# The triangular inverse of a 128-token chunk, made from its two 64x64 diagonal blocks on opposite quarters of TensorE

## The chip, the cores and the metric

The kernel runs on one core of one Trainium2 chip. The metric is the device time of one execution in microseconds, the median of several runs. The engines of a core are TensorE (PE in the profile; its weight loads are PEld), VectorE (DVE), ScalarE (ACT), GpSimd (POOL) and SyncE (SP), which issues DMAs. Each works through its own list of instructions in order and waits for others by semaphores.

## The reference

One layer of a streaming encoder over 2048 tokens of width 1024: an RMS norm, one wide projection, a gated delta rule (8 heads of width 128, with a short causal convolution and a decay), a sliding-window attention with sinks, their gated merge, an output projection and a last norm. The part that the change touches is the triangular inverse inside the delta rule, per head and per chunk of 64 tokens:

```
n_mat = where(strict_lower, -(kb @ k.T) * decay, 0)
t_mat = eye + n_mat
p_mat = n_mat
for _ in range(log2(CHUNK) - 1):        # CHUNK = 64
    p_mat = p_mat @ p_mat
    t_mat = t_mat + t_mat @ p_mat       # ends as inverse(I - n_mat)
u = t_mat @ vb
w = t_mat @ (kb * exp(gc))
```

A state of 128x128 per head is then carried from chunk to chunk.

## The kernel before

The 2048 tokens are worked on in 4 blocks of 512 (`NB`), a block in 8 heads, a head in 4 chunks of 128 tokens (`NT`, twice the reference's chunk, which gives the same outputs). All weights come as tiles of 128x1024. In block 0 a tile arrives in float32 and is split into a high part (ScalarE, L436) and a low part (POOL, L363); both are saved, and later blocks load them back. A weight product is three passes (L1074 to L1076: high by high, high by low, low by high) for each of eight slices of the contraction.

TensorE's list is written out by hand. While it works on the delta rule and the attention of one head, it also projects the next head's inputs: six weight tiles (q, k and v of the delta rule, the attention's query, two gates) of eight steps each, 48 steps of three matmuls. `fill(n)` in the head's code runs the next n of these steps, and `fill(99)` all that are left. The last head of a block fills with six gate tiles instead. Two PSUM banks (0 and 1) take the projected tiles in turn, so that a tile's first step waits (`z_read`) until the tile two before has been read out of its bank. ScalarE and VectorE have fill steps of their own in their lists, which read these banks: ScalarE copies the projections (L518, L542, L543) and takes the tanh of the gates (L551), VectorE does the convolution (L840, L844) and the SiLU (L826).

A head begins with the sums of decays (L1161), transposes of k, q and v (L1157), and the products k by k and q by k (L1168). VectorE makes the negated strict triangle from k by k, transposed, in `pt_sb[0]` (L886), for four chunks side by side in a 128x512 tile, and adds the identity (L890). After nine fill steps TensorE transposes this (L1225), and ScalarE copies it to `p_sb[0]` (L589). Then come six levels (`LEVELS`). `square(l)` makes the next power of the triangle (L1179) and its transpose (L1183), four 128x128 float32 products each; ScalarE copies both (L589, L595). `accumulate(l)` multiplies the running inverse by that power (L1193), and VectorE adds the result (L905). The attention's logits (L1203), the transposes of its probabilities (L1210) and its values (L1218) stand between the levels, and one or two fill steps between any two of them.

Then the four chunks of 128 tokens are run through the state in order (L1256 to L1272), with fill steps between, and `fill(99)`. In that time VectorE normalizes the head's output (L988) by a power that POOL computes (L376). The head ends when TensorE transposes this output (L1282); `head_dve_done` says that VectorE has gated it. `square_o` (L650) sums the squares of the outputs on ScalarE; for the last chunk it stands ahead of ScalarE's remaining fill steps.

Of the kernel before, what the change touches and what calls it, by code (L numbers as in the profile page):

```python
# [6 lines left out]
P = 128  # L7
# [3 lines left out]
TB = 512  # L11
# [10 lines left out]
LEVELS = 6  # L22
# [77 lines left out]
def build_program(nc, x, w_tiles, norm_w, gdn_norm_w, decay_bias, step_const, bias, final_w, masks, saved, out):  # L100
    with ExitStack() as ctx:
# [79 lines left out]
        p_sb = [chunks(scratch(4)), chunks(scratch(5))]  # L181
        pt_sb = [chunks(scratch(6)), chunks(scratch(7))]
        tt_sb = [chunks(scratch(8)), chunks(scratch(9))]
# [83 lines left out]
        attn_ready = sem("attn_ready")  # L267
        p_done = sem("p_done")
        pt_done = sem("pt_done")
        tt_done = sem("tt_done")  # L270
        p_ready = sem("p_ready")
        pt_ready = sem("pt_ready")
        tt_ready = sem("tt_ready")
        s0_ready = sem("s0_ready")
# [143 lines left out]
        def _(act):  # L418
# [151 lines left out]
            def head(par, n1, fill):  # L570
                n4, n5, n7 = ((n1 - 1) * i for i in (NT, LEVELS - 1, LEVELS + 1))
# [26 lines left out]
                squares(ssq[:, 1, :], bch(3), ssq_ready[1], 1, tt_sb[1])  # L598
                act.wait_ge(dec_done, n1)
                act.activation(dec, bch(5), ACT.Exp).then_inc(dec_ready, 1)  # L600
                squares(ssq[:, 0, :], bch(2), ssq_ready[0], 0, p_sb[1])
                act.wait_ge(ssq_ready[1], n1)
                fill(1)
                p_copy(0)
# [5 lines left out]
                pt_copy(1)  # L610
# [4 lines left out]
                pt_copy(2)  # L615
# [14 lines left out]
                pt_copy(3)  # L630
                softmax_exp(0)
                p_copy(4)
                pt_copy(4)
                p_copy(5)
                pt_copy(5)
                probs_copy(0)
                fill(1)
                p_copy(6)
# [9 lines left out]
                def square_o(t):  # L648
                    act.wait_ge(o_ready, n4 + (t + 1))
                    ins = act.activation(tt_sb[1][:, t, :], o_sb[:, t, :], ACT.Square, accum_out=sso[:, t:t + 1])  # L650
                    if t == NT - 1:
                        ins.then_inc(sso_ready, 1)
# [86 lines left out]
        def _(dve):  # L739
# [122 lines left out]
            def head(b, hh, fill):  # L862
                par, n1 = hh % 2, b * H + hh + 1
                n4, n6, n7 = ((n1 - 1) * i for i in (NT, LEVELS, LEVELS + 1))
# [20 lines left out]
                for t in range(NT):  # L885
                    ins = dve.scalar_tensor_tensor(pt_sb[0][:, t, :], bch(6)[:, t, :], bj[:, t:t + 1], dec_n[:, t, :],  # L886
                                                   ALU.mult, ALU.mult)
                ins.then_inc(pt_ready, 1)
                dve.wait_ge(pt_ready, n6 + 1)
                dve.tensor_tensor(tt_sb[0], pt_sb[0], mk[:, IDENT:IDENT + 1, :].to_broadcast([P, NT, P]), ALU.add  # L890
                                  ).then_inc(tt_ready, 1)
# [56 lines left out]
                add_tt(6)  # L948
# [122 lines left out]
        def _(pe):  # L1071
# [78 lines left out]
            def head(b, par, n1, fill):  # L1150
                n4, n6, n7 = ((n1 - 1) * i for i in (NT, LEVELS, LEVELS + 1))
# [20 lines left out]
                fill(9)  # L1172
# [13 lines left out]
                def accumulate(l):  # L1186
# [3 lines left out]
                    if l == 1:  # L1190
                        pe.wait_ge(attn_ready, n1)
# [258 lines left out]
```

## Time and profile before

| | |
|---|---|
| Median of 3 runs | 3073.92 us (3073.32 to 3075.18) |
| Profiled execution | 3076.6 us |
| Its span, first to last instruction | 3074.8 us |
| TensorE matmul busy | 2972.8 us, 97% |
| TensorE weight load busy | 2541.9 us, 83% |
| VectorE busy | 1401.3 us, 46% |
| ScalarE busy | 1052.9 us, 34% |
| POOL busy | 415.6 us, 14% |
| Granted TensorE clock, mean | 0.997 of full speed |

Matmuls are pipelined: a record lasts from its start to its modelled end, and the next begins before that. What a matmul costs in a row of equal ones is therefore the time from start to start. A row of the timeline merges equal instructions that follow each other on an engine: its start, its length, and their number as x8. An idle time in brackets is that of the engine ahead of the row, with what ended it.

### The profile page before, as it was taken

Reading aid. Unit: us, or ns where it says so; the run is one execution under the profiler, and the core shown is the slowest. Engines: PE = TensorE matmul, PEld = TensorE weight load, DVE = VectorE, ACT = ScalarE, POOL = GpSimd, SP = SyncE. Lnnn points to the kernel's source line nnn. Section 1 sums busy time; section 2 is a strip of 40 time slices with the busy share of each in tenths; the row PEclk is TensorE's granted clock in tenths of the full one; section 3 lists DMA queues with packets and bytes.
Section 4 is the critical chain, followed back from the end, with each engine's and each line's share of the span. In section 5 each row is a group of like instructions: output and inputs, shape, how many; then the busy total and the mean of one; then the engine's idle time right before and its main releaser. Section 6 shows DMA issues by size and latency. Waiting matters only on the chain.

```text
span 3074.8 us, 44670 instructions
## 1 busy us (share of the span) xinstructions
PE 2972.8 (97%) x17576; PEld 2541.9 (83%) x17576; DVE 1401.3 (46%) x2949; ACT 1052.9 (34%) x2993; POOL 415.6 (14%) x237
## 2 busy tenths in 40 slices
PE   6999999999999999999999999999999999999997
PEld 5888887888888888888888888888888888888886
DVE  4676666523255555532235555552223555554112
ACT  3444444432234434331114433343112343343100
POOL 3332233343201000100000000100000001100000
PEclk9999999999999999999999999999999999999998
DMA  6444343488633222345562222324555223222463
GB/s 224 163 167 146 126 144 134 158 296 313 231 143 110 88 99 98 112 150 206 192 222 98 86 105 104 114 97 165 213 185 194 98 98 112 102 96 97 170 223 140
DMA packets 77535, 462.85 MB, mean 151 GB/s; under 512 B 13072, under 2 KB 17296, under 8 KB 29200
## 3 DMA queue, kind: packets, MB, share of 16 engines
q1 hardware_dynamic: 65520, 429.42, 39.2%
q10 hardware_dynamic: 11808, 30.57, 2.7%
q8 instruction: 141, 2.31, 0.3%
q14 instruction: 66, 0.54, 0.1%
HBM read 356.15 MB, written 103.81 MB: 150 GB/s over the span
## 4 chain that ended last, share of the span: by engine, by line
PE 83%; issue 9%; DVE 5%; ACT 3%; DMA 0%; POOL 0%; DVEq 0%; POOLq 0%; SPq 0%
PE bank L1074 18%; PE bank L1076 18%; PE bank L1075 18%; PE bank L1179 6%; PE bank L1193 5%; PE bank L1183 5%; PE bank L1203 2%; PE bank L1168 2%; ACT area L621 1%; PE bank L1157 1%; PE bank L1264 1%; PE bank L1218 1%; PE bank L1256 1%; PE bank L1210 1%; DVE area L844 1%
## 5 line engine op out<-in xcount | busy, mean ns | idle before, releaser
L1074 PE MATMUL bank<-hT_hi,w_sl 128*128 128x512 f32 x2144 | 897.8, 419 | 1.4 <-DVE hT_lo L768 1.3
L1076 PE MATMUL bank<-hT_hi,w_sl 128*128 128x512 f32 x2144 | 840.2, 392 | 0.0
L1075 PE MATMUL bank<-hT_lo,w_sl 128*128 128x512 f32 x2144 | 837.3, 391 | 0.0
L1076 PEld LDWEIGHTS bank<-hT_hi,w_sl 128*128 128x128 f32 x2144 | 402.4, 188 | 88.2
L1074 PEld LDWEIGHTS bank<-hT_hi,w_sl 128*128 128x128 f32 x2144 | 404.7, 189 | 65.8 <-ACT hT_hi L462 2.1
L1075 PEld LDWEIGHTS bank<-hT_lo,w_sl 128*128 128x128 f32 x2144 | 405.3, 189 | 58.7
L905 DVE TENSOR_TENSOR area<-bank,area 128x512 f32<-128x512 f32 x192 | 132.7, 691 | 415.9 <-PE bank L1193 415.9
L363 POOL TENSOR_TENSOR w_sl<-w_raw,w_sl 128x1024 fp32r<-128x1024 f32 x91 | 219.2, 2409 | 525.3 <-ACT w_sl L436 525.3
L844 DVE SCALAR_TENSOR_TENSOR area<-zraw,stc,area 128x512 f32<-128x512 f32 x288 | 232.6, 808 | 4.3
L1179 PEld LDWEIGHTS bank<-area 128*128 128x128 f32 x1536 | 198.2, 191 | 29.7 <-issue 15.6
L376 POOL TENSOR_TENSOR rqo<-qo,half 128x8 f32<-128x8 f32 x32 | 64.6, 2018 | 1076.7 <-DVE qo L983 1076.7
L1179 PE MATMUL bank<-area 128*128 128x128 f32 x1536 | 204.6, 276 | 2.5
L589 ACT ACTIVATE area<-bank 128x512 f32<-128x512 f32 x224 | 133.7, 597 | 208.3 <-PE bank L1179 197.6
L1193 PE MATMUL bank<-area 128*128 128x128 f32 x1536 | 202.8, 275 | 0.0
L1193 PEld LDWEIGHTS bank<-area 128*128 128x128 f32 x1536 | 189.2, 192 | 2.9 <-issue 0.2
L436 ACT ACTIVATE w_sl<-w_raw 128x1024 fp32r<-128x1024 f32 x91 | 96.1, 1056 | 225.1 <-PE bank L1076 176.8
L1183 PE MATMUL bank<-area 128*128 128x128 f32 x1280 | 169.1, 275 | 0.0
L1183 PEld LDWEIGHTS bank<-area 128*128 128x128 f32 x1280 | 155.8, 192 | 0.0
L643 ACT ACTIVATE o_sb<-bank,scs 128x128 f32<-128x128 f32 x128 | 47.1, 368 | 250.8 <-PE bank L1261 250.8
L960 DVE SCALAR_TENSOR_TENSOR s_cur<-s_cur,scs,bank 128x128 f32<-128x128 f32 x128 | 44.2, 346 | 150.2 <-PE bank L1269 150.2
L595 ACT ACTIVATE area<-bank 128x512 f32<-128x512 f32 x160 | 95.5, 597 | 45.2 <-PE bank L1183 45.2
L646 ACT ACTIVATE y_sb<-bank 128x128 f32<-128x128 f32 x128 | 35.5, 278 | 219.6 <-PE bank L1264 219.4
(183 smaller groups left out, 4511.4 us busy)
## 6 DMA issues: line engine op xcount, KB each, us to landing
w_sl<-saved_w SPq DMA_DIRECT2D x273, 1024.0 KB, 4.8
saved_w<-w_sl SPq DMA_DIRECT2D x91, 1024.0 KB, 4.8
w_raw<-in_w_tiles SPq DMA_DIRECT2D x91, 512.0 KB, 5.7
area<-in_x ACTq DMA_DIRECT2D x8, 2048.0 KB, 10.1
out_y<-area ACTq DMA_DIRECT2D x4, 2048.0 KB, 7.3
bias_sb<-in_bias ACTq DMA_DIRECT2D x33, 128.0 KB, 3.0
fw<-in_final_w ACTq DMA_DIRECT2D x1, 512.0 KB, 10.1
stc<-in_step_const ACTq DMA_DIRECT2D x32, 6.5 KB, 2.3
```

Of the source, the lines that this page charges most:

```text
L363: pool.tensor_tensor(w_sl[:, s, 1, :], w_raw[:, f % 2, :], w_sl[:, s, 0, :].bitcast(F32), ALU.subtract).then_inc(lo_ready, 1)
L436: act.activation(w_sl[:, s, 0, :], w_raw[:, f % 2, :], ACT.Copy).then_inc(hi_ready, 1)
L589: act.activation(p_sb[l % 2], bch(5), ACT.Copy).then_inc(p_ready, 1)
L595: act.activation(pt_sb[l % 2], bch(6), ACT.Copy).then_inc(pt_ready, 1)
L844: ins = dve.scalar_tensor_tensor(acc, zraw[:, i, k:k + TB], stc[:, par, CONV * i + k:CONV * i + k + 1], acc, ALU.mult, ALU.add)
L905: dve.tensor_tensor(tt_sb[l % 2], bch(7), tt_sb[(l - 1) % 2], ALU.add).then_inc(tt_ready, 1)
L1074: pe.matmul(dst, a_hi, b_hi, start=first, stop=False)
L1075: pe.matmul(dst, a_hi, b_lo, start=False, stop=False)
L1076: return pe.matmul(dst, a_lo, b_hi, start=False, stop=last)
L1179: ins = pe.matmul(bch(5)[:, t, :], pt_sb[(l - 1) % 2][:, t, :], p_sb[(l - 1) % 2][:, t, :], start=True, stop=True)
L1183: ins = pe.matmul(bch(6)[:, t, :], p_sb[(l - 1) % 2][:, t, :], pt_sb[(l - 1) % 2][:, t, :], start=True, stop=True)
L1193: ins = pe.matmul(bch(7)[:, t, :], p_sb[l % 2][:, t, :], tt_sb[(l - 1) % 2][:, t, :], start=True, stop=True)
```

## The change

The 128x128 unit triangle to be inverted is cut into four blocks of 64x64. With A and B its diagonal blocks, the diagonal blocks of the inverse are the inverses of A and B, and the one corner block is a product of these two and the old corner.

- The diagonal blocks of a chunk stand at rows 0 to 63 and 64 to 127 of a 64-column tile (`ptt`, `p_sb`), so that the two products of a chunk use rows and columns 0 to 63 and 64 to 127 of TensorE's array. `square(l)` makes the next power with eight products of 64x64x64.
- `apply(l)` replaces the transposed square and `accumulate`: `ptt` holds the transposed power in its columns 0 to 63 and the running inverse in columns 64 to 127, and one product per block of 64 by 128 moves both on by a level. Level 1 has no inverse to move yet, level 6 no power.
- There are five squares (`LEVELS` is 5) and six applies.
- The copy of the transposed power goes from ScalarE to VectorE (`level`), with half the columns; each copy and addition now takes 256 columns, not 512. ScalarE's first copy becomes five of 256 columns: two of the diagonal blocks of the transposed triangle, two of those of the triangle, and one of the corner block (`od`).
- `merge_in` multiplies the corner by one inverse and transposes the other by a product with the identity (eight products); after two copies `merge_out` makes the corner of the inverse (four products), and VectorE copies it into `tt`.
- The fill steps move: 8 ahead of the transposes (9 before), then 2, 1, 2, 2, 2, 1, 2, 2 and 1 up to the state's first product (before 2 and seven times 1); after that as before.
- The scratch tiles that only take unused outputs of the sums of squares get other names.

```diff
-LEVELS = 6
+LEVELS = 5
...
+        HALVES = ((0, CH), (CH, P))
...
 # ScalarE
-                    act.wait_ge(p_done, n7 + (l + 1))
-                    act.activation(p_sb[l % 2], bch(5), ACT.Copy).then_inc(p_ready, 1)
-
-                def pt_copy(l):
-                    act.wait_ge(pt_done, n5 + l)
-                    if l == 2:
-                        act.wait_ge(tt_ready, n7 + 1)
-                    act.activation(pt_sb[l % 2], bch(6), ACT.Copy).then_inc(pt_ready, 1)
+                    act.wait_ge(p_done, n6 + (l + 1))
+                    if l:
+                        act.activation(p_sb[l % 2], pv(bank[5]), ACT.Copy).then_inc(p_ready, 1)
+                    else:
+                        for lo, hi in HALVES:
+                            act.activation(p_sb[0][lo:hi], bch(5)[lo:hi, :, lo:hi], ACT.Copy)
+                        act.activation(od[CH:P], bch(5)[CH:P, :, 0:CH], ACT.Copy).then_inc(p_ready, 1)
...
                 fill(1)
+                act.wait_ge(f_ready, n1)
+                for lo, hi in HALVES:
+                    ins = act.activation(ptt[lo:hi, :, 0:CH], tt[lo:hi, :, lo:hi], ACT.Copy)
+                ins.then_inc(pt0_ready, 1)
                 p_copy(0)
...
-                p_copy(6)
+                act.wait_ge(tz_done, n1)
+                act.activation(t11[0:CH], bch(7)[0:CH, :, 0:CH], ACT.Copy).then_inc(t11_ready, 1)
 # VectorE
-                def add_tt(l):
-                    dve.wait_ge(tt_ready, n7 + l)
-                    dve.wait_ge(tt_done, n6 + l)
-                    dve.tensor_tensor(tt_sb[l % 2], bch(7), tt_sb[(l - 1) % 2], ALU.add).then_inc(tt_ready, 1)
+                def level(l):
+                    dve.wait_ge(a_done, n6 + l)
+                    if l < LEVELS:
+                        copy(ptt[:, :, 0:CH], bch(6)[:, :, 0:CH]).then_inc(pt_ready, 1)
+                    if l > 1:
+                        dve.wait_ge(tt_ready, n5 + l - 1)
+                        dve.tensor_tensor(ptt[:, :, CH:P], bch(6)[:, :, CH:P], ptt[:, :, CH:P], ALU.add).then_inc(tt_ready, 1)
+
+                def diagonal():
+                    dve.wait_ge(a_done, n6 + (LEVELS + 1))
+                    dve.wait_ge(tt_ready, n5 + LEVELS)
+                    for lo, hi in HALVES:
+                        ins = dve.tensor_tensor(tt[lo:hi, :, lo:hi], bch(6)[lo:hi, :, CH:P], ptt[lo:hi, :, CH:P], ALU.add)
+                    ins.then_inc(diag_ready, 1)
+
+                def corner():
+                    dve.wait_ge(t12_done, n1)
+                    copy(tt[0:CH, :, CH:P], bch(6)[0:CH, :, 0:CH]).then_inc(full_ready, 1)
...
-                fill(2)
-                add_tt(1)
+                fill(1)
+                level(1)
+                fill(1)
+                level(2)
                 logits(0)
-                add_tt(2)
+                level(3)
                 fill(1)
-                add_tt(3)
+                level(4)
                 quotient(0)
+                level(5)
                 fill(1)
-                add_tt(4)
-                add_tt(5)
+                diagonal()
                 gated(0)
+                dve.wait_ge(tz_done, n1)
+                copy(z_sb[0:CH], bch(5)[0:CH, :, 0:CH]).then_inc(z_ready, 1)
                 fill(1)
-                add_tt(6)
+                corner()
 # TensorE
-                fill(9)
+                fill(8)
...
                     for t in range(NT):
-                        ins = pe.matmul(bch(5)[:, t, :], pt_sb[(l - 1) % 2][:, t, :], p_sb[(l - 1) % 2][:, t, :], start=True, stop=True)
+                        for lo, hi in HALVES:
+                            ins = pe.matmul(pv(bank[5])[lo:hi, t, :], ptt[lo:hi, t, 0:CH], p_sb[(l - 1) % 2][lo:hi, t, :], start=True, stop=True)
                     ins.then_inc(p_done, 1)
...
+                def apply(l):
+                    pe.wait_ge(p_ready, n6 + l)
+                    c0, c1 = (0 if l < LEVELS else CH), (P if l > 1 else CH)
+                    if l > 1:
+                        pe.wait_ge(tt_ready, n5 + l - 1)
                     for t in range(NT):
-                        ins = pe.matmul(bch(7)[:, t, :], p_sb[l % 2][:, t, :], tt_sb[(l - 1) % 2][:, t, :], start=True, stop=True)
-                    ins.then_inc(tt_done, 1)
+                        for lo, hi in HALVES:
+                            ins = pe.matmul(bch(6)[lo:hi, t, c0:c1], p_sb[(l - 1) % 2][lo:hi, t, :], ptt[lo:hi, t, c0:c1], start=True, stop=True)
+                    ins.then_inc(a_done, 1)
+
+                def merge_in():
+                    pe.wait_ge(attn_ready, n1)
+                    pe.wait_ge(diag_ready, n1)
+                    for t in range(NT):
+                        pe.matmul(bch(7)[0:CH, t, 0:CH], tt[0:CH, t, 0:CH], ident[0:CH, 0:CH], start=True, stop=True)
+                        ins = pe.matmul(bch(5)[0:CH, t, 0:CH], od[CH:P, t, :], tt[CH:P, t, CH:P], start=True, stop=True)
+                    ins.then_inc(tz_done, 1)
+
+                def merge_out():
+                    pe.wait_ge(t11_ready, n1)
+                    pe.wait_ge(z_ready, n1)
+                    for t in range(NT):
+                        ins = pe.matmul(bch(6)[0:CH, t, 0:CH], t11[0:CH, t, :], z_sb[0:CH, t, :], start=True, stop=True)
+                    ins.then_inc(t12_done, 1)
...
                 fill(2)
                 square(1)
+                apply(1)
                 fill(1)
                 square(2)
-                accumulate(1)
+                apply(2)
                 logits(0)
-                fill(1)
+                fill(2)
                 square(3)
-                accumulate(2)
-                fill(1)
+                apply(3)
+                fill(2)
                 square(4)
-                accumulate(3)
-                fill(1)
+                apply(4)
+                fill(2)
                 square(5)
-                accumulate(4)
+                apply(5)
                 probs(0)
                 fill(1)
-                square(6)
-                accumulate(5)
+                apply(6)
                 values(0)
+                fill(2)
+                merge_in()
+                logits(1)
+                fill(2)
+                merge_out()
                 fill(1)
-                accumulate(6)
-                logits(1)
-                fill(1)
...
                     pe.wait_ge(r_ready, n4 + (t + 1))
+                    if t == 0:
+                        pe.wait_ge(full_ready, n1)
```

## Rows read from the trace of the kernel before

**Rows 1.** The page: its span, busy times and the chain that ended last.
```profile
span 3074.8 us, 44670 instructions
...
PE 2972.8 (97%) x17576; PEld 2541.9 (83%) x17576; DVE 1401.3 (46%) x2949; ACT 1052.9 (34%) x2993; POOL 415.6 (14%) x237
...
PE 83%; issue 9%; DVE 5%; ACT 3%; DMA 0%; POOL 0%; DVEq 0%; POOLq 0%; SPq 0%
```

**Rows 2.** Windows, from:to and length, busy us, clock: one head, seven of block 0.
```profile
986.24:1050.28 64.04, 62.66 (x417) 54.54 (x416) 34.60 (x82) 25.77 (x84) 5.75 (x4) 1.00 0.29 101
...
87.91:553.65 465.74, 445.10 (x2899) 380.26 (x2898) 314.87 (x570) 218.68 (x623) 143.95 (x70) 1.00 0.42 144
```

**Rows 3.** Timeline of TensorE (start, length, line), without and with the attention's values.
```profile
1010.41 1.06 PE L1193 MATMUL bank<-area 128*128 128x128 f32 x8
...
1011.53 0.40 PE L1075 MATMUL bank<-hT_lo,w_sl 128*128 128x512 f32 x1
...
1015.81 1.05 PE L1179 MATMUL bank<-area 128*128 128x128 f32 x8
1016.70 1.06 PE L1193 MATMUL bank<-area 128*128 128x128 f32 x8
1017.69 0.69 PE L1218 MATMUL bank<-area,vwin 128*64 128x64 f32 x16
...
1018.64 0.39 PE L1075 MATMUL bank<-hT_lo,w_sl 128*128 128x512 f32 x1
```

**Rows 4.** Timeline of the weight loads in the same stretch.
```profile
1017.69 0.55 PEld L1218 LDWEIGHTS bank<-area,vwin 128*64 128x64 f32 x16
```

**Rows 5.** Timeline of TensorE and of ScalarE around the first squares of a head.
```profile
998.18 1.05 PE L1179 MATMUL bank<-area 128*128 128x128 f32 x8
...
1000.43 0.40 PE L1076 MATMUL bank<-hT_hi,w_sl 128*128 128x512 f32 x1
1000.91 1.13 PE L1179 MATMUL bank<-area 128*128 128x128 f32 x8
...
995.93 0.60 ACT L518 ACTIVATE zraw<-bank 128x512 f32<-128x512 f32 x1 [5.54 <-PE bank L1076]
996.99 0.60 ACT L589 ACTIVATE area<-bank 128x512 f32<-128x512 f32 x1 [0.46 <-PE bank L1225]
997.48 1.13 ACT L584 ACTIVATE area<-bank,ksc 128x128 f32<-128x128 f32 x4
```

**Rows 6.** Groups of VectorE's instructions in that head: count, busy us, mean ns.
```profile
L844 DVE SCALAR_TENSOR_TENSOR area<-zraw,stc,area 128x512 f32<-128x512 f32 x9 | 6.7, 747 | 0.1
L905 DVE TENSOR_TENSOR area<-bank,area 128x512 f32<-128x512 f32 x6 | 4.1, 692 | 13.1 <-PE bank L1193 13.1
...
L934 DVE TENSOR_TENSOR zb<-bank,zb 128x256 f32<-128x256 f32 x2 | 0.8, 424 | 0.3 <-PE bank L1218 0.3
```

**Rows 7.** Timeline of three engines at the end of the same head.
```profile
1040.04 0.39 PE L1272 MATMUL bank<-y_sb,area 128*128 128x128 f32 x2
...
1040.96 0.40 PE L1074 MATMUL bank<-hT_hi,w_sl 128*128 128x512 f32 x1
...
1049.84 0.60 PE L1282 MATMUL bank<-mk,area 128*128 128x128 f32 x4
...
1041.79 0.59 ACT L543 ACTIVATE qbd<-bank 64x512 f32<-64x512 f32 x1
...
1044.15 0.69 DVE L988 TENSOR_TENSOR area<-area,fo 128x512 f32<-128x512 f32 x1
```

**Rows 8.** Timeline of a head of block 0: a weight rounding, and its end.
```profile
431.23 1.06 ACT L436 ACTIVATE w_sl<-w_raw 128x1024 fp32r<-128x1024 f32 x1 [4.71 <-PE bank L1076]
...
484.08 2.89 DVE L988 TENSOR_TENSOR area<-area,fo 128x512 f32<-128x512 f32 x1
...
487.12 0.63 PE L1282 MATMUL bank<-mk,area 128*128 128x128 f32 x4
```

**Rows 9.** TensorE's waits: who for whom, us in total, times, longest.
```profile
PE bank L1256 <- DVE area L905: 2.4, 7, 0.3
```

More of the change, by code:

```diff
@@ L180, in build_program, with blocks @@
         dec_n = chunks(scratch(3))
-        p_sb = [chunks(scratch(4)), chunks(scratch(5))]
-        pt_sb = [chunks(scratch(6)), chunks(scratch(7))]
-        tt_sb = [chunks(scratch(8)), chunks(scratch(9))]
+        HALVES = ((0, CH), (CH, P))
+        def blocks(ap):
+            return ap.rearrange("p (t c) -> p t c", t=NT)
+        p_sb = [blocks(area2[:, 4 * TB:4 * TB + NT * CH]), blocks(area2[:, 4 * TB + NT * CH:5 * TB])]
+        z_sb = p_sb[0]
+        ptt = chunks(scratch(5))
+        od = blocks(area2[:, 6 * TB:6 * TB + NT * CH])
+        t11 = blocks(area2[:, 6 * TB + NT * CH:7 * TB])
+        tt = chunks(scratch(8))
+        junk_q, junk_k = chunks(scratch(7)), chunks(scratch(9))
         attn = dec
@@ L570, in head @@
             def head(par, n1, fill):
-                n4, n5, n7 = ((n1 - 1) * i for i in (NT, LEVELS - 1, LEVELS + 1))
+                n4, n6 = ((n1 - 1) * i for i in (NT, LEVELS + 1))
                 sc = scs[:, par, :, :]
@@ L863, in head @@
                 par, n1 = hh % 2, b * H + hh + 1
-                n4, n6, n7 = ((n1 - 1) * i for i in (NT, LEVELS, LEVELS + 1))
+                n4, n5, n6 = ((n1 - 1) * i for i in (NT, LEVELS, LEVELS + 1))
                 ch = Chain(dve, dve_head, (n1 - 1) * DVE_HEAD)
@@ L1150, in head @@
             def head(b, par, n1, fill):
-                n4, n6, n7 = ((n1 - 1) * i for i in (NT, LEVELS, LEVELS + 1))
+                n4, n5, n6 = ((n1 - 1) * i for i in (NT, LEVELS, LEVELS + 1))
                 q, k, vv = (qkv[:, par, i, :] for i in range(3))
@@ L1180, in square @@
                     ins.then_inc(p_done, 1)
-                    if l < LEVELS:
-                        for t in range(NT):
-                            ins = pe.matmul(bch(6)[:, t, :], p_sb[(l - 1) % 2][:, t, :], pt_sb[(l - 1) % 2][:, t, :], start=True, stop=True)
-                        ins.then_inc(pt_done, 1)
-                def accumulate(l):
-                    pe.wait_ge(p_ready, n7 + (l + 1))
-                    pe.wait_ge(tt_ready, n7 + l)
-                    if l == 1:
-                        pe.wait_ge(attn_ready, n1)
-                    for t in range(NT):
-                        ins = pe.matmul(bch(7)[:, t, :], p_sb[l % 2][:, t, :], tt_sb[(l - 1) % 2][:, t, :], start=True, stop=True)
-                    ins.then_inc(tt_done, 1)
+                def apply(l):
+                    pe.wait_ge(p_ready, n6 + l)
+                    c0, c1 = (0 if l < LEVELS else CH), (P if l > 1 else CH)
+                    if l > 1:
+                        pe.wait_ge(tt_ready, n5 + l - 1)
+                    for t in range(NT):
+                        for lo, hi in HALVES:
+                            ins = pe.matmul(bch(6)[lo:hi, t, c0:c1], p_sb[(l - 1) % 2][lo:hi, t, :], ptt[lo:hi, t, c0:c1], start=True, stop=True)
+                    ins.then_inc(a_done, 1)
@@ L1222, in head @@
                 pe.wait_ge(dec_ready, n1)
[L1223 removed]
+                pe.wait_ge(f_ready, n1)
                 for t in range(NT):
[L1225 removed]
+                    ins = pe.transpose(bch(5)[:, t, :], tt[:, t, :], ident)
                 ins.then_inc(p_done, 1)
```

43 lines of the change are left out of this document (22 added, 21 removed).

## The prediction

> **What bounds the kernel now.** I read the page first. TensorE is busy 97% of the span and the chain that ended last is 83% TensorE, with VectorE and ScalarE at 5% and 3% [rows 1]. What counts is therefore TensorE's own time, and the waits of others only where they stop it. Next I cut the span into heads, from one decay product (L1161) to the next [rows 2]. The head from 986.24 to 1050.28 takes 64.04 us, of which TensorE is busy 62.66 at a granted clock of 1.00. The stretch of the first seven heads of block 0 takes 465.74 us, 66.5 per head: there POOL and ScalarE also split fresh weights (POOL is busy 143.95 us). VectorE is busy 34.60 us of the 64.04 and ScalarE 25.77, so both have room on average, and only their order can hurt.
>
> The inverse now takes six levels of three groups (squares, transposed squares, accumulations), 6 + 5 + 6 = 17 groups per head, each of four 128x128 float32 products. Every product shows as two records, so that a group is a row of eight; they take from 1015.81 to 1016.70, 0.89 us, 111 ns per record [rows 3]. 17 x 0.89 = 15.13 us per head.
>
> **What a group on quarters costs.** The trace of before has no 64x64 quarter. Its nearest rows are the attention values (L1218): 64 columns on two halves of the array, all 128 rows, eight products, 16 records. Their weight loads take 0.55 us together [rows 4], less one of 0.14 over 15 steps: 27.5 ns per record. The matmuls take 0.69, less one of 0.22, over 15: 31 ns. One such record alone should need half of 111 ns, 55. So the two halves run side by side. But entering and leaving costs: from the start of the accumulation at 1016.70 to the second weight product (L1075) at 1018.64 is 1.94 us; the same way without values, 1010.41 to 1011.53, is 1.12 [rows 3]. The values thus fill 0.82, while 16 x 31 ns are 0.50: 0.32 per visit goes to filling and draining the array.
>
> I take these for the quarters: 31 ns a record at 64 moving columns (16 records, 0.50), 55.5 ns at 128 (16 records, 0.89), and 0.32 per visit. From both sides: if two quarters don't overlap, 55.5 and 111 ns; if nothing is paid for the visit, 0. I take the middle since the values share everything with the new products but the split of the rows.
>
> Per head after the change, in visits:
> - level 1, eight squares and eight applies at 64 columns: 0.50 + 0.50 + 0.32 = 1.32
> - levels 2 to 5, squares at 64 and applies at 128: 0.50 + 0.89 + 0.32 = 1.71, four times 6.84
> - level 6, the last apply, which runs straight into the values: 0.50 + 0.16
> - the corner: eight products at 0.50 + 0.32, then four that all stand on one quarter: 8 x 55.5 ns + 0.32 = 0.76
>
> The sum is 10.40 us against 15.13: TensorE saves 4.73 us per head although it issues 100 products where it issued 68.
>
> **Waits.** Each fill step is three weight products, 0.69 us: fourteen of them and a drain lie between the last product of the state at 1040.04 and the transposes at 1049.84 [rows 7]. There are 48 per head in both kernels (six weight tiles of eight steps). What changes is where they stand.
>
> (a) The wait before the second square goes. The step before it starts its last product at 1000.43, so the square could start 0.23 later, and starts at 1000.91 [rows 5]: 0.25 lost. It waits for a 512-wide copy of the transposed square, third in ScalarE's queue. That copy now is 256 wide and on VectorE.
>
> (b) A wait before the first square comes. The transposes (L1225) move one fill step earlier, so TensorE is ready for it 0.69 earlier, at 997.49 by the times of this head [rows 5]. ScalarE can't follow: its copy of the projection (L518) waits for the eighth step and starts at 995.93 all the same, and behind it now stand two copies of the transposed block and three of the transposes, where one copy stood. From start to start a copy of 512 columns takes 0.49 (996.99 to 997.48), and one of 128 some 0.25 (four in 1.13, the last 0.38 long) [rows 5]; for 256 I take 0.33, with a duration of 0.42 at most. Five make 1.65 us after 996.42, and the square starts at about 998.15: +0.65. In block 0 a weight rounding of 1.06 stands ahead of L518 [rows 8]: I take +1.6 there.
>
> (c) The other levels have cover. Between two squares lie an apply, two fill steps (1.38) or, at level 2, the logits as well. What must fit in is a drain of about 0.2, ScalarE's 0.42 at most and VectorE's 0.42 for 256 columns [rows 6], twice at levels 2 to 4. VectorE gets 14 operations of 0.42 (5.9 us) for 7 of 0.69 (4.8), ScalarE 11 of 0.42 for 12 of 0.60. The narrowest place is before square 2: one fill step (0.69), the drain and 0.42, behind a convolution step. Without cover each miss costs at most one VectorE fill step, 0.75 [rows 6]. The merge has two fill steps ahead of each half, and the finished matrix is first needed three steps after that.
>
> (d) At the end of a head the moved steps come back as a wait. Ahead of the first state product now stand 23 of the 48 steps, before 18; after each token chunk's products as before 17 more. So 40 steps are done after the last state product, where 35 were, and step 41 opens the sixth weight tile. Its PSUM bank must have been read by ScalarE's two query copies (L542, L543), and these stand behind the square of the last output in ScalarE's queue: the second runs from 1041.79 to 1042.38 [rows 7]. Step 40 would end where the first step after the last state product ends now, at 1040.96 [rows 7]. TensorE waits until about 1042.45: +1.48 in heads 0 to 6 of a block. Before, step 41 came five steps later and found the bank free. Eight steps from there end at 1047.95; the normalized output (L988) is there at 1044.84 [rows 7], so that the transposes are then next and late for nothing else. Head 7 fills with gates, which ScalarE reads one by one in time, and has no such wait.
>
> (e) In block 0 the tail is not TensorE's. There the normalized output ends at 486.97 and the transposes start at 487.12 [rows 8]: POOL's weight splits run beside it, and the normalization there takes 2.89 us where it takes 0.69 in the later head [rows 7, 8]. Five steps taken from this tail don't shorten it, so their 5 x 0.69 = 3.45 is lost again in heads 0 to 6; (d) vanishes within it. A wait of about 0.35 on the last addition of the old inverse, seen seven times [rows 9], goes there.
>
> **The sum**, against the profiled execution's span:
> - blocks 1 to 3, heads 0 to 6: -4.73 - 0.25 + 0.65 + 1.48 = -2.85, times 21 = -60
> - blocks 1 to 3, head 7: -4.73 - 0.25 + 0.65 = -4.33, times 3 = -13
> - block 0, heads 0 to 6: -4.73 - 0.25 - 0.35 + 1.60 + 3.45 = -0.28, times 7 = -2
> - block 0, head 7: -4.73 - 0.25 - 0.35 + 1.60 = -3.7
>
> Together -79. The span of 3074.8 becomes 2996, the execution of 3076.6 some 2998; that execution lies 2.7 us above the median of 3073.9, so against the median 2995. Some 151 us of TensorE time go, and about half is given back.
>
> **Rivals.**
>
> Quarters take turns. If two quarters can't write one PSUM bank at a time, every pair of squares and applies goes one by one: 16 records take 0.89 at 64 columns and 1.78 at 128. Level 1 is then 2.10, levels 2 to 5 are 2.99 each, the rest 0.89 + 0.16 + 1.21 + 0.76: 17.1 us per head, 1.95 more than now. With (a) to (e), heads cost +3.83 (21), +2.35 (3), +6.4 (7) and +3.0: +135, or 3209. It decides from the first level on; the change turns slower once a pair takes more than some 70% of two turns, where the line between -79 (half) and +135 (all) crosses zero. For it: the new pairs differ in rows, which the values do not, and both halves of a pair write one bank. Against it: the values' two halves also write one bank at different partitions, and overlap [rows 3, 4].
> The Trainium skill speaks for this rival: TensorEngine Tiling (Array Packing), section Restrictions and Gotchas, says that different row tiles cannot access the same PSUM bank at once. No row here shows two row tiles. By that rule the time would be the 3209 of this rival.
>
> The visits are free. If going to quarters and back costs nothing where the weight products around them keep the queue full, 0.32 x 7.5 = 2.4 us less per head in all 32: 2995 - 77 = 2918. For it: the drain of 0.32 was read at one kind of row only. Against: that row is the same switch.
>
> VectorE's queue is late. The transposed square, until now ScalarE's, is queued behind convolution steps (0.75) and the softmax's maximum. If two levels of a head each wait 0.75, 1.5 x 32 = 48 more: 3043. Against: 34.60 busy of 64.04 [rows 2] and two fill steps of cover at levels 3 to 5.
>
> **How the numbers follow.** Forecast (quarters overlap, visits cost, tail gives half back) 0.58, with a range of its own from 2960 to 3030; turns 0.17; free visits 0.12; late VectorE queue 0.13, which with the forecast's worst ends reaches 3085 at most. The range leaves out the turns and a little below: 2900 to 3085. Faster by over 0.2% (6 us), the least that a measurement of this kernel tells from no change: 0.58 + 0.12 + most of 0.13, 0.79. Within: 0.04. Slower: 0.17.
>
> **What would show it.** The squares' 16 records in 0.5 to 0.6 us and the applies' 16 in about 0.9; twice that means turns. A gap ahead of each visit and behind it, together 0.3. Heads of blocks 1 to 3 at about 61.1 us, of block 0 near 66. A wait of TensorE on ScalarE's query copies of 1.5 us in 21 heads or more, and one of 0.5 on the copies ahead of the first square. The forecast falls if heads 0 to 6 and head 7 save the same, if waits stand before squares 2 to 5, or if the clock in the heads leaves 1.00.

## The result and the profile after

The changed kernel takes 2984.06 us (median of 4, 2981.82 to 2985.61), the kernel before 3074.55 in the same runs (3073.32 to 3076.43): a ratio of 0.9707, 95% interval 0.9695 to 0.9718. Forecast were 2995 us, within 2900 to 3085. The profiled executions are 94.8 us of span apart.

The page of the changed kernel, against [rows 1]: TensorE's share of the chain falls from 83% to 77%, and ScalarE's rises from 3% to 7%.

```profile
span 2980.0 us, 48798 instructions
...
PE 2802.1 (94%) x19624; PEld 2275.4 (76%) x19624; DVE 1416.4 (48%) x3173; ACT 957.2 (32%) x2961; POOL 414.9 (14%) x237
...
PE 77%; issue 9%; ACT 7%; DVE 5%; POOL 1%; DMA 0%; DVEq 0%; POOLq 0%; ACTq 0%; SPq 0%
```

TensorE is busy 170.7 us less, and the span is 94.8 shorter: some of what was saved has become idle time. Windows of the changed kernel, with the columns of [rows 2]: the same head (head 2 of block 1, counted from 0; it begins at 966.20 here), the first seven heads of block 0, and the last heads of blocks 0 and 1, each with the work up to the next block's first head (before: 304.57 and 302.12 us).

```profile
966.20:1027.04 60.84, 57.42 (x481) 46.20 (x480) 35.64 (x89) 22.79 (x83) 5.76 (x4) 1.00 0.30 107
88.25:545.42 457.17, 407.38 (x3348) 323.65 (x3346) 305.14 (x619) 198.59 (x616) 141.79 (x70) 1.00 0.43 147
...
545.42:844.55 299.13, 297.07 (x1562) 245.07 (x1561) 103.14 (x174) 94.84 (x181) 100.63 (x44) 1.00 0.74 262
1270.37:1567.73 297.36, 296.63 (x1562) 245.23 (x1561) 86.54 (x174) 57.48 (x143) 7.41 (x6) 1.00 0.54 195
```

The head went from 64.04 to 60.84 us. Its TensorE busy time fell by 5.24 and its idle time rose from 1.4 to 3.4. The granted clock is 1.00 in all four. The seven heads of block 0 lost 8.57 us, 1.22 each. TensorE's waits say where the idle time is (engine and line, who is waited for, us in total, times, longest; against [rows 9]):

```profile
PE bank L1107 <- ACT qbd L559: 45.9, 28, 2.3
...
PE bank L1216 <- ACT area L610: 30.3, 32, 1.8
...
PE bank L1335 <- DVE area L1021: 5.4, 6, 0.9
```

All three rows are new. The first is a weight step on ScalarE's query copies in 28 heads, the second the first square on ScalarE's copies in all 32, the third the transposes at the end of a head on the normalized output, in six heads of block 0. The old wait on the last addition of the inverse [rows 9] is gone, and no square or apply after the first waits for anyone.

TensorE in the head from 966.20, with the end of the head ahead of it (start, length, line):

```profile
958.43 0.40 PE L1109 MATMUL bank<-hT_hi,w_sl 128*128 128x512 f32 x1
960.22 0.47 PE L1107 MATMUL bank<-hT_hi,w_sl 128*128 128x512 f32 x1 [1.39 <-ACT qbd L559]
...
977.24 0.40 PE L1109 MATMUL bank<-hT_hi,w_sl 128*128 128x512 f32 x1
978.34 0.68 PE L1216 MATMUL bank<-area 64*64 64x64 f32 x16 [0.71 <-ACT area L610]
...
979.76 0.40 PE L1108 MATMUL bank<-hT_lo,w_sl 128*128 128x512 f32 x1
...
983.97 0.40 PE L1109 MATMUL bank<-hT_hi,w_sl 128*128 128x512 f32 x1
984.29 0.68 PE L1216 MATMUL bank<-area 64*64 64x64 f32 x16
984.81 1.04 PE L1227 MATMUL bank<-area 64*64 64x128 f32 x16
...
986.12 0.39 PE L1108 MATMUL bank<-hT_lo,w_sl 128*128 128x512 f32 x1
...
990.12 0.39 PE L1109 MATMUL bank<-hT_hi,w_sl 128*128 128x512 f32 x1
990.43 0.68 PE L1216 MATMUL bank<-area 64*64 64x64 f32 x16
990.95 0.63 PE L1227 MATMUL bank<-area 64*64 64x64 f32 x16
991.51 0.66 PE L1261 MATMUL bank<-mk,area 128*128 128x128 f32 x4
```

Read it so. A level's cost is the time from the start of the last weight product ahead (L1109) to the second one behind (L1108), less the two paces of 0.23 (0.45 together) that stand there without it. Level 3, from 983.97 to 986.12, costs 2.15 - 0.45 = 1.70; the forecast had 1.71. The squares' 16 records take 0.52 from start to start (984.29 to 984.81), 32 ns each. The quarters run side by side. Level 5, the last four rows, moves 64 columns in its apply; no weight product stands behind it, so its end is the start of L1261 and one pace goes off: 1.39 - 0.23 = 1.16, not 1.71.

### The profile page after: what moved, and what is told of

It is laid out like the page before. It is cut to its first block, busy times and chain, and to the rows that moved or that the text cites. A ratio compares the mean times of both kernels' runs of the same rounds, so it can differ in the third digit from the quotient of the medians.

```text
span 2980.0 us, 48798 instructions
## 1 busy us (share of the span) xinstructions
PE 2802.1 (94%) x19624; PEld 2275.4 (76%) x19624; DVE 1416.4 (48%) x3173; ACT 957.2 (32%) x2961; POOL 414.9 (14%) x237
## 4 chain that ended last, share of the span: by engine, by line
PE 77%; issue 9%; ACT 7%; DVE 5%; POOL 1%; DMA 0%; DVEq 0%; POOLq 0%; ACTq 0%; SPq 0%
PE bank L1107 19%; PE bank L1109 18%; PE bank L1108 18%; PE bank L1227 4%; PE bank L1216 3%; PE bank L1254 2%; PE bank L1201 2%; ACT area L637 1%; PE bank L1190 1%; PE bank L1269 1%; PE bank L1317 1%; PE bank L1261 1%; PE bank L1307 1%; PE bank L1194 1%; DVE area L858 1%
## 5 line engine op out<-in xcount | busy, mean ns | idle before, releaser
L1109 PE MATMUL bank<-hT_hi,w_sl 128*128 128x512 f32 x2144 | 841.2, 392 | 0.0
L1108 PE MATMUL bank<-hT_lo,w_sl 128*128 128x512 f32 x2144 | 839.0, 391 | 0.0
L1109 PEld LDWEIGHTS bank<-hT_hi,w_sl 128*128 128x128 f32 x2144 | 402.9, 188 | 89.9
L1108 PEld LDWEIGHTS bank<-hT_lo,w_sl 128*128 128x128 f32 x2144 | 405.5, 189 | 57.1
L379 POOL TENSOR_TENSOR w_sl<-w_raw,w_sl 128x1024 fp32r<-128x1024 f32 x91 | 221.6, 2435 | 514.1 <-ACT w_sl L452 514.1
L757 DVE TENSOR_SCALAR area<-bank 128x256 f32<-128x256 f32 (+1 forms) x192 | 81.0, 422 | 302.6 <-PE bank L1227 186.6
L392 POOL TENSOR_TENSOR rqo<-qo,half 128x8 f32<-128x8 f32 x32 | 64.6, 2020 | 1037.1 <-DVE qo L1016 1037.1
L452 ACT ACTIVATE w_sl<-w_raw 128x1024 fp32r<-128x1024 f32 x91 | 96.0, 1055 | 218.0 <-PE bank L1109 146.5
L1227 PE MATMUL bank<-area 64*64 64x128 f32 (+1 forms) x3072 | 162.4, 245 | 0.0
L1216 PEld LDWEIGHTS bank<-area 64*64 64x64 f32 x2560 | 87.1, 134 | 90.5 <-issue 46.4
L1227 PEld LDWEIGHTS bank<-area 64*64 64x64 f32 x3072 | 134.7, 134 | 11.8 <-issue 11.8
L606 ACT ACTIVATE area<-bank 128x256 f32<-128x256 f32 x160 | 62.0, 388 | 240.7 <-PE bank L1216 240.7
L1216 PE MATMUL bank<-area 64*64 64x64 f32 x2560 | 109.0, 224 | 30.3 <-ACT area L610 30.3
L1057 DVE SCALAR_TENSOR_TENSOR area<-area,bank 128x512 f32<-128x512 f32 x28 | 19.2, 688 | 185.9 <-PE bank L1109 185.9
L1107 PE MATMUL bank<-w_sl,oa_hi 128*128 128x512 f32 x256 | 100.6, 393 | 0.0
L1107 PE MATMUL bank<-oa_hi,w_sl 128*128 128x512 f32 x256 | 100.2, 391 | 0.0
```

What stands on the lines that cost most here:

```text
L379: pool.tensor_tensor(w_sl[:, s, 1, :], w_raw[:, f % 2, :], w_sl[:, s, 0, :].bitcast(F32), ALU.subtract).then_inc(lo_ready, 1)
L392: pool.tensor_tensor(dst, src, half[:, 0:n], ALU.pow).then_inc(ready, 1)
L452: act.activation(w_sl[:, s, 0, :], w_raw[:, f % 2, :], ACT.Copy).then_inc(hi_ready, 1)
L606: act.activation(p_sb[l % 2], pv(bank[5]), ACT.Copy).then_inc(p_ready, 1)
L757: return dve.tensor_scalar(dst, src, 1.0, None, ALU.mult)
L1107: pe.matmul(dst, a_hi, b_hi, start=first, stop=False)
```

## The experiments

The theory: the quarters overlap because neighbours in the list stand on different quarters, a visit costs about 0.33 us, and most of what is lost again goes with the five moved steps (the wait on the query copies, and the tail of block 0) and with the order of ScalarE's copies. The rivals: TensorE reorders its products so far that their order doesn't matter; the longer fills between the levels are needed as cover, so that the steps can't go back without new waits; and visits cost nothing. The kernel before ran beside each group of experiments, at 3074.15 and 3074.02 us; ratios are against it, and differences against the change's 2984.06 us.

### Quarters one after the other

```diff
-                    for t in range(NT):
-                        for lo, hi in HALVES:
+                    for lo, hi in HALVES:
+                        for t in range(NT):
```

in `square` and `apply`: the same products, but four chunks on one quarter and then four on the other.

> The eight products of a square or an apply in another order: first the four chunks on the first quarter, then the four on the second, so that neighbours stand on the same quarter. Same products, same waits. Theory (the quarters of a pair run side by side, and a pair takes the time of one): neighbours on one quarter take turns, 55 ns a record at 64 columns and 111 at 128 where the changed kernel shows 30 and 55. Per head 5 squares and 3 applies of 64 columns each 0.4 us longer, 3 applies of 128 columns each 0.9 longer: 5.9 us, in all 32 heads about 185 us, so 3165 to 3175, slower than the first kernel. Rival (a 64x64 product is cheap by its size, not by its neighbour): no change, 2984. Rival (TensorE reorders enough to overlap them in any order): within 20 us of 2984.

Measured: 3080.33 us, ratio 1.0024 (1.0015 to 1.0033), 96 above the change. The order alone undoes the whole gain, but the size is half of what was expected. Level 3 in this kernel's timeline of TensorE:

```profile
1022.27 0.79 PE L1216 MATMUL bank<-area 64*64 64x64 f32 x13
1022.85 0.32 PE L1227 MATMUL bank<-area 64*64 64x128 f32 x1
1022.90 0.28 PE L1216 MATMUL bank<-area 64*64 64x64 f32 x2
1023.01 0.27 PE L1227 MATMUL bank<-area 64*64 64x128 f32 x1
1023.02 0.22 PE L1216 MATMUL bank<-area 64*64 64x64 f32 x1
1023.12 1.31 PE L1227 MATMUL bank<-area 64*64 64x128 f32 x14
1024.36 0.50 PE L1107 MATMUL bank<-hT_hi,w_sl 128*128 128x512 f32 x1
```

The first apply record, on the low quarter, starts at 1022.85 while the last three records of the squares, all on the high quarter and all ahead of it in the list, have still to start. So TensorE does take a product of the idle quarter before its turn, but here only near the border between the runs. The level lasts from 1022.27 to 1024.36, 2.09 us, where full turns would be 2.66 (16 x 0.0555 and 16 x 0.111) and the change has 1.49. The theory is right in kind, since the overlap needs neighbours on different quarters, and wrong in size: TensorE reorders enough to save about half of it.

### ScalarE's copies ahead of its fill step

```diff
-                fill(1)
                 act.wait_ge(f_ready, n1)
                 ...                            # the two copies of the transposed triangle
+                fill(1)
                 p_copy(0)
```

> ScalarE's two copies of the transposed block moved ahead of its fill step, into time in which it is idle in the changed kernel (5 us before the projection's copy); three copies are left behind that fill step. Theory (the first square waits for ScalarE's five copies in a row): the wait of the first square falls by two copies of 0.33, from about 0.9 to 0.25 us in blocks 1 to 3 and from 1.8 to 1.15 in block 0, so 32 x 0.65 = 21 us less: 2963. Rival (the gap is TensorE's own switch to quarters): unchanged, 2984.

Measured: 2960.50 us, ratio 0.9632 (0.9619 to 0.9645), 23.6 below the change. ScalarE in the changed kernel, ahead of the first square of the head above:

```profile
975.90 0.60 ACT L534 ACTIVATE zraw<-bank 128x512 f32<-128x512 f32 x1 [5.53 <-PE bank L1109]
976.39 0.83 ACT L620 ACTIVATE area<-area 64x256 f32<-64x256 f32 x2
977.25 0.77 ACT L609 ACTIVATE area<-bank 64x256 f32<-64x256 f32 x2
977.92 0.37 ACT L610 ACTIVATE area<-bank 64x256 f32<-64x256 f32 x1
```

ScalarE had been idle for 5.53 us, waiting for a projection (L534). Moved ahead of it, the two copies of L620 run inside that gap, and the wait on the copies stands in block 0 alone. The waits of TensorE in the edited kernel:

```profile
PE bank L1216 <- ACT area L610: 9.5, 8, 1.7
```

Eight times instead of 32. The head's window falls to 60.05 us, 0.79 less; the heads of block 0 fall by 0.4 on average.

### The moved steps put back

Five of the longer fills return to one step, so that five steps stand again at the end of the head:

```diff
                 logits(0)
-                fill(2)
+                fill(1)
                 square(3)
...              # the same behind apply(3), apply(4), values(0) and logits(1)
```

> Five of the fill steps that the change moved ahead of the state go back to the head's end: one less after the first logits, after applies 3 and 4, after the values and after the second logits. 18 of 48 steps then stand ahead of the state, as in the first kernel. Theory (the moved steps come back as the wait for the query copies in blocks 1 to 3, and in block 0 as a tail that POOL and VectorE set; the levels have cover for one step): the wait of 1.5 us per head goes in blocks 1 to 3 (21 heads, -32), block 0 gets 3.4 us per head back (7 heads, -24), new waits inside the levels of at most 0.2 us a head (+6): 2934, between 2925 and 2945. Rival (the steps were moved because the shorter levels no longer cover the copies): each of five steps that is gone uncovers about 0.5 us in every head, +80, less 56: 3008.

Measured: 2919.17 us, ratio 0.95 (0.9487 to 0.9513), 65 below the change. Windows of a head of block 0 and of the steady head in this kernel:

```profile
150.14:211.58 61.44, 57.55 (x481) 46.15 (x480) 43.64 (x89) 28.44 (x88) 20.40 (x10) 1.00 0.45 157
937.50:996.56 59.06, 57.05 (x480) 46.28 (x479) 35.64 (x89) 22.87 (x83) 5.75 (x4) 1.00 0.32 110
```

The steady head loses 1.78 us, of which the wait on the query copies and its restart are 1.64. The head of block 0, the second, loses 3.5 (it takes 64.90 in the changed kernel), five steps of 0.69; over the seven it is 3.7 on average. No wait between the levels appears: the longer fills were not needed as cover, and that rival falls. The gain is 15 us above the expectation: the 6 us of new waits did not come, the 21 steady heads gave 5 us more than the wait alone, and block 0 gave 2 more; the rest is the place of the profiled execution among the runs.

### The same move without the inverse

The kernel before, with its fill steps moved to the places they have in the change:

```diff
-                fill(9)
+                fill(8)
...
-                fill(1)      # ahead of squares 3, 4 and 5
+                fill(2)
...
                 values(0)
-                fill(1)
+                fill(3)
                 accumulate(6)
                 logits(1)
-                fill(1)
+                fill(2)
```

> The first kernel, with its inverse of 128x128 products, in which only the fill steps are moved as far as in the change: 8 ahead of the transposes and 23 of the 48 ahead of the state's first product. Theory (what the change gives back comes from the moved steps alone): in blocks 1 to 3 step 41 waits for ScalarE's query copies, 1.6 us in 21 heads, and some 0.15 to get going again, +36; in block 0 the tail is set by the normalized output, 3.45 us lost in 7 heads, +24: 3134, between 3122 and 3142. Rival (steps are steps: what stands ahead is saved behind; the gain of putting them back lay in the shorter inverse): 3074 within 6.

Measured: 3137.45 us, ratio 1.0208 (1.0194 to 1.0222): 63 us slower with the old inverse, as putting the steps back made the new one 65 faster. The wait is the same to the digit; the waits of TensorE in this kernel:

```profile
PE bank L1074 <- ACT qbd L543: 45.9, 28, 2.3
```

A steady head of it takes 65.73 us (before 64.04), and the first seven heads of block 0 lose 3.7 on average, what they gained above. So the loss belongs to the place of the steps and not to the quarters.

### The query copies ahead of the last square of the output

```diff
                 square_o(2)
+                fill(1)
                 square_o(3)
```

in ScalarE's list.

> On ScalarE the next head's query copies, and in block 0 the weight rounding ahead of them, come before the square of the head's last output, not behind it. Theory (step 41 waits for these copies, which wait only for their place in ScalarE's list): ScalarE is idle for a microsecond there, so the copies end by 1 us earlier: the wait of 1.6 us falls to at most 0.2 in 21 heads of blocks 1 to 3, -30 us. In block 0 POOL's split starts 1 us earlier and the square of the last output 1.2 later, so the tail moves by -1 to +1 us in 7 heads. 2954, between 2945 and 2962. Rival (step 41 waits for something else, or the normalized output is next at once): less than 10 us gained, 2975 or more.

Measured: 2934.32 us, ratio 0.9549 (0.9536 to 0.9562), 50 below the change, 20 more than expected. In the steady head it did what was expected (59.43 us, 1.4 less). The miss is block 0, where nothing was expected and the heads fall by 2.5 us, from 64.88 to 62.40. ScalarE, POOL and VectorE at the end of the first head, first in the changed kernel:

```profile
143.79 1.04 ACT L452 ACTIVATE w_sl<-w_raw 128x1024 fp32r<-128x1024 f32 x1
144.91 2.37 POOL L379 TENSOR_TENSOR w_sl<-w_raw,w_sl 128x1024 fp32r<-128x1024 f32 x1 [9.25 <-ACT w_sl L452]
147.24 2.08 POOL L392 TENSOR_TENSOR rqo<-qo,half 128x8 f32<-128x8 f32 x1
...
149.58 2.40 POOL L379 TENSOR_TENSOR w_sl<-w_raw,w_sl 128x1024 fp32r<-128x1024 f32 x1 [0.26 <-ACT w_sl L452]
149.63 2.90 DVE L1021 TENSOR_TENSOR area<-area,fo 128x512 f32<-128x512 f32 x1
```

and then in the edited one:

```profile
142.18 1.05 ACT L452 ACTIVATE w_sl<-w_raw 128x1024 fp32r<-128x1024 f32 x1
143.31 2.37 POOL L379 TENSOR_TENSOR w_sl<-w_raw,w_sl 128x1024 fp32r<-128x1024 f32 x1 [7.86 <-ACT w_sl L452]
145.98 2.07 POOL L392 TENSOR_TENSOR rqo<-qo,half 128x8 f32<-128x8 f32 x1 [0.30 <-DVE qo L1017]
...
148.35 0.69 DVE L1022 TENSOR_TENSOR area<-area,fo 128x512 f32<-128x512 f32 x1
149.09 2.78 POOL L379 TENSOR_TENSOR w_sl<-w_raw,w_sl 128x1024 fp32r<-128x1024 f32 x1 [1.05 <-ACT w_sl L452]
```

TensorE's wait on the query copies is down to 0.9 us from 2.3 in this block. The fill step that was moved holds, in block 0, the weight rounding (L452) as well: against the head's start (88.25 and 88.04) it is 1.4 us earlier, and so is POOL's weight split (L379), which waits for it. So the split is out of the way of the power operation (L392), and the next split no longer starts beside VectorE's normalization, which takes 0.69 instead of 2.90. TensorE's wait on the normalized output is gone from heads 0 to 6.

### Twice the visits

Levels 3 and 4 with a fill step between square and apply: two visits more per head, the same work.

```diff
                 square(3)
+                fill(1)
                 apply(3)
-                fill(2)
+                fill(1)
...              # the same at level 4
```

> At levels 3 and 4 one of the two fill steps behind the apply now stands between the square and the apply: the same products and the same number of steps, but TensorE goes to the quarters and back twice more per head, 64 times more in all. Theory (going to quarters and back costs TensorE about 0.3 us): 64 x 0.3 = 19 us more, 3003, with no new wait at squares 4 and 5, since one step of cover was enough in the kernel with the steps put back. Rival (the switch is free; the gaps in the trace are only how the ends of matmuls are drawn): 2984 within 4. Rival (one step no longer covers the copies): 0.4 us more for each of 64 places and a wait of TensorE on VectorE's or ScalarE's copy, 3010 to 3030.

Measured: 3005.46 us, ratio 0.9777 (0.9763 to 0.979). 21.4 us over 64 visits are 0.33 us per visit, as read from one other kind of row before (0.32). The waits of TensorE on ScalarE stay as they were (30.3 us in 32 heads, all at the first square), and no apply waits, so uncovered copies are not the cause. What in the switch takes the time, the runs do not show.

### Both mends together, and all three

The second and third experiments in one kernel (their two diffs):

> The two edits together: the copies of the transposed block ahead of ScalarE's fill step, and five fill steps back at the head's end. Theory (they are different waits at different ends of the head, so the gains add): 2919 less the 23.5 that the copies gave alone, 2896, between 2891 and 2901. Rival (TensorE, freed at the first square, meets a wait further on): 2905 to 2919.

Measured: 2895.51 us, ratio 0.9419 (0.9406 to 0.9432). 88.6 us below the change is the sum of the two alone (23.6 + 64.9): they don't share a place. It is the fastest kernel here.

Then the query copies ahead of the last square as well, in all heads but the last of a block:

```diff
                 square_o(2)
+                if n1 % H:
+                    fill(1)
                 square_o(3)
```

> As the one with copies and steps, and ScalarE's query copies ahead of the square of the last output, in all heads but a block's last. Theory (with the steps back, step 41 finds its bank free anyway; what is left is block 0, where POOL's split starts earlier and the tail, 9.95 us by the normalized output, becomes the 9.67 of TensorE's own steps): 0.3 x 7 = 2 us less than with copies and steps, 2894. Rival (the query copies were still on the path): 20 or more less, 2875.

Measured: 2899.95 us, ratio 0.9434 (0.9421 to 0.9447). This is a miss: 4.4 us slower than without it, and not 2 faster. POOL and VectorE at the start of the third head, in the kernel with two mends:

```profile
210.83 0.43 DVE L1028 TENSOR_SCALAR oa_hi<-za 128x512 fp32r<-128x512 f32 x1
...
211.99 2.37 POOL L379 TENSOR_TENSOR w_sl<-w_raw,w_sl 128x1024 fp32r<-128x1024 f32 x1 [3.31 <-ACT w_sl L452]
```

and with three:

```profile
210.99 2.36 POOL L379 TENSOR_TENSOR w_sl<-w_raw,w_sl 128x1024 fp32r<-128x1024 f32 x1 [1.61 <-ACT w_sl L452]
211.08 2.56 DVE L1030 TENSOR_SCALAR oa_hi<-za 128x512 fp32r<-128x512 f32 x1
```

In the first head, which meets no such collision at its start, the tail did get shorter, by the 0.3 us that were expected (60.54 to 60.23). The six heads behind it take 0.45 to 0.7 more. With the third mend an earlier weight split, of the head before, ends at 203.15 instead of 204.00, and SyncE then issues the load of a later tile (203.55, before 204.39). That tile lands at 209.59 instead of 210.79, ScalarE rounds it at 209.86 instead of 210.86, and its split now starts just ahead of VectorE's rounding of the gated output, which takes 2.56 us instead of 0.43. TensorE's transposes wait for that rounding's successor; the waits of TensorE in the kernel with three:

```profile
PE bank L1192 <- DVE oa_lo L1031: 4.4, 7, 0.6
```

That is 4.4 us in seven heads, where the kernel with two mends has this wait once, 0.6 long. The steady heads have no weight split and stay at 58.3 us with or without the third mend.

## Why the prediction was right, and where its sizes were off

**The quarters.** They overlap, on which the forecast and its 0.58 rested; the rival "quarters take turns" falls with the squares' 32 ns a record. The forecast took 31 ns from the attention's values, which share the rows; the new pairs split them, and it makes no difference.

**The groups of the inverse: 10.40 forecast, 9.56 measured.** The columns below are the visits of one head, each read as level 3 was above.

| visit | forecast | measured |
|---|---|---|
| level 1 (wait left out) | 1.32 | 1.19 |
| level 2 | 1.71 | 1.58 |
| levels 3 and 4 | 3.42 | 3.40 |
| level 5 | 1.71 | 1.16 |
| level 6 | 0.66 | 0.71 |
| corner, in and out | 0.82 + 0.76 | 0.70 + 0.82 |

The step that failed is level 5: the forecast let all of "levels 2 to 5" move 128 columns. The code takes `c0 = CH` from `l == LEVELS` on, and `LEVELS` is now 5, so that not only level 6's apply, as the description of the change has it, but level 5's too leaves the power out. The groups of the changed kernel, by shape, show it: three of six levels at each width (1536 records are 48 a head, 16 a level).

```profile
L1227 PE MATMUL bank<-area 64*64 64x128 f32 x1536 | 100.1, 269 | 0.0
...
L1227 PE MATMUL bank<-area 64*64 64x64 f32 x1536 | 62.3, 220 | 0.0
```

That is 0.39 us per head and 12.5 over 32 heads, of the 16 by which the forecast of -79 fell short of the spans' -95. Most of the other 0.45 are the exits: behind levels 2 and 5 and the first corner products stands no weight product but another small one (L1254, L1261), and those visits cost 0.12 to 0.16 less than 0.32 would make them. Level 1's entry is counted with its wait.

**(a) and (c), the second square and the cover.** As forecast. The second square waits no more, and nothing waits in levels 2 to 5, although VectorE now makes the transposed copies. The rival of VectorE's late queue falls.

**(b) The first square.** It waits 0.87 us, not 0.65: TensorE could start it 0.23 after 977.24 and does at 978.34. Five copies of 256 columns take 1.92 (976.39 to 978.31), 0.38 each; the forecast put 0.33 between two paces read from [rows 5]. In block 0 TensorE idles 1.64 us there in heads 0 to 6 and 1.8 in head 7, where the steady head idles 0.71 of its 0.87; the forecast had 1.6 lost.

**(d) The query copies.** The step that should start at 958.66 starts at 960.22: 1.56 us, forecast 1.48, at the step forecast (the 41st). It comes in 28 heads, as heads 0 to 6 of four blocks have it.

**(e) Block 0.** The five steps return nothing, as forecast, but not only for the reason given. The forecast let the wait of (d) vanish within a tail that the normalization sets. In six of the seven heads TensorE does wait for the normalized output, but for 0.9 us; on the query copies it idles 2.3 in all seven, and their place in ScalarE's list also delays a weight split and the power operation behind it, so that the normalization meets the next split. Moved ahead, they return 2.5 us in the first head with all five steps left where they are. The heads of block 0 gain 1.22 us each, forecast 0.28; 0.84 of the difference is that of the groups.

**The sum.** In a steady head the terms as measured are -5.57 (15.13 to 9.56) - 0.25 + 0.87 + 1.56 = -3.39, and the head moved by -3.20 (64.04 to 60.84). Of what is left, 0.2, the slow first product after the stall (0.31 to the next instead of 0.23) is 0.08; the rest has no place. Over the program: 21 x -3.20 = -67 (forecast -60), three last heads -14 (-13), block 0 -8.6 and -5.4 (-2 and -3.7), together -95 against -94.8 of the spans.

**Where the rest went.** The inverse itself saves about 178 us (5.57 x 32). The moved steps give back 65 (shown twice, with either inverse), of which ScalarE's order at the end of a head alone returns 50; the first-square wait is 30 of idle time (its row above), and the order of ScalarE's copies alone returns 24. The visits, 7.5 x 0.33 x 32 = 79 us, are within the 9.56 and are still paid by all versions; the rival "visits are free" falls with the doubled visits. Whether the squares and applies of two heads could share a visit was not tried.

## What to carry to other kernels

Small products on opposite quarters of TensorE pay in full only if neighbours in its list stand on different quarters (1.49 us a level here, 2.09 with the quarters one after the other), and each trip from whole-array products to quarters and back costs 0.33 us here, so make few trips. Filler work that is moved forward to cover a wait is taken from the place where it covered another: ask what the steps at the end of the loop were hiding before they are taken away. A mend that shortens one wait can move other work into a collision, as the third one here did, so mends are tried together and not only added up. An engine in a hand-written list that waits for late data, with ready work behind it, is a mend of two lines (24 us).

## What was not expected of the hardware

**Two quarters in one PSUM bank.** The first corner products stand on two lines, so that the records of a pair show apart (timeline of TensorE in the changed kernel):

```profile
995.72 0.22 PE L1235 MATMUL bank<-mk,area 64*64 64x64 f32 x1
995.73 0.22 PE L1236 MATMUL bank<-area 64*64 64x64 f32 x1
995.78 0.22 PE L1235 MATMUL bank<-mk,area 64*64 64x64 f32 x1
```

The two of a pair start 0.01 us apart, and pairs follow at 0.06. These two write different banks; the squares write one bank from both quarters and are as fast (16 records in 0.52). So the bank cost nothing here, and the rule that the prediction weighed does not hold for this pair of row tiles, which write different partitions. The Trainium skill has a narrower form that agrees: in PSUM — Partial Sum Buffer, section PSUM bank collisions raise a hardware error, which also quotes the broad rule, two writes of TensorE from different row tiles are measured to collide in one bank and quadrant (32 partitions). The squares' two quarters write partitions 0 to 63 and 64 to 127 and so no common quadrant.

**Products out of the list's order.** In the kernel with quarters one after the other, records of a later line start ahead of three earlier ones of the other quarter (1022.85 against 1022.90 to 1023.02). So the description ahead of the prediction, by which each engine works through its list in order, does not hold for TensorE between two quarters here.

**POOL beside VectorE.** A rounding on VectorE that starts 0.09 us after a weight split on POOL ends 0.29 after it and takes 2.56 us, not 0.43. The Trainium skill, SBUF — State Buffer, section SBUF: two separate sides, calls the port pair of the two an exclusive lock and not a shared bandwidth; the trace agrees, since the rounding, after 2.27 us beside the split, still takes 0.29 of its 0.43 behind it, and the normalization above, in the changed kernel (149.63 to 152.53), 0.55 of its 0.69 behind the split that ends at 151.98.
